# Dilated attention's six query and key projections as three seven-product groups, with their norm weights applied by ScalarE

## What is computed

```python
h = rms_norm_2(x, norm_w)                      # 256 x 1024
q, k, v = h @ w_in[...]                        # each 256 x (3 groups x 8 heads x 64)
q = rms_norm_2(q, q_norm_w)                    # over the 64 channels of a head, weight per group
k = rms_norm_2(k, k_norm_w)
q, k = apply_partial_rope(q), apply_partial_rope(k)   # channels 0 to 15 of 64 are rotated
```

## Time and profile before

| | |
|---|---|
| median of 3 runs | 939.36 us (938.86 to 939.88) |
| the profiled execution's own time | 938.56 us |
| its span in the profile | 936.6 us |
| TensorE matmuls busy | 925.4 us (99%) |
| VectorE busy | 699.5 us (75%) |
| ScalarE busy | 235.3 us (25%) |
| GpSimd busy | 40.6 us (4%) |
| granted TensorE clock | 1.0 of 2.4 GHz |

### The profile page before, as it was taken

One profiled execution on the slowest core, in us unless ns is written; L12 is line 12 of the kernel. 1 busy time (PEld: TensorE's weight loads), 2 busy tenths in 40 slices (PEclk: granted clock), 3 DMA queues, 4 the chain that ended last, 5 costly groups with the idle time before them and its releaser, 6 DMA issues.

```text
span 936.6 us, 12484 instructions
## 1 busy us (share of the span) xinstructions
PE 925.4 (99%) x4976; PEld 583.6 (62%) x4976; DVE 699.5 (75%) x1218; ACT 235.3 (25%) x473; POOL 40.6 (4%) x59
## 2 busy tenths in 40 slices
PE   7999999999999999999999999999999999999998
PEld 5954555945555459999744459457864444469444
DVE  4875965589658677958899763988978789674676
ACT  5314422233333222332100011311103212323210
POOL 0500000000005300000000000000000000000000
PEclk9999999999999999999999999999999999999999
DMA  9753441553527524435555536522424344231721
GB/s 335 243 182 121 149 134 45 180 180 104 189 91 176 185 94 177 142 131 181 180 180 179 179 126 233 181 91 94 177 90 179 111 159 181 94 131 47 269 90 45
DMA packets 51960, 141.77 MB, mean 151 GB/s; under 512 B 4320, under 2 KB 8320, under 8 KB 51648
## 3 DMA queue, kind: packets, MB, share of 16 engines
q1 hardware_dynamic: 49152, 134.55, 40.9%
q0 software_dynamic: 2144, 5.84, 2.6%
q10 hardware_dynamic: 608, 0.61, 0.2%
HBM read 138.89 MB, written 2.10 MB: 151 GB/s over the span
## 4 chain that ended last, share of the span: by engine, by line
PE 98%; DMA 0%; ACT 0%; DVE 0%; issue 0%; DVEq 0%; ACTq 0%
PE pair L2207 34%; PE pair L2292 26%; PE pair L2288 16%; PE pair L2557 6%; PE turned L2148 4%; PE score L2557 3%; PE turned L2557 1%; PE score L2650 1%; PE score L2450 1%; PE score L2466 1%; PE score L2393 1%; PE score L2394 1%; PE score L2719 1%; PE turned L2637 0%; DMA ident<-in_c_ident 0%; PE score L2299 0%
## 5 line engine op out<-in xcount | busy, mean ns | idle before, releaser
L2207 PE MATMUL pair<-ring,hT 128*128 128x512 f32 (+2 forms) x512 | 214.0, 573 | 0.9 <-ACT hT L718 0.9
L1137 DVE TENSOR_TENSOR arena<-arena 128x512 f32<-128x512 f32 (+5 forms) x324 | 192.0, 607 | 17.7 <-PE score L2557 4.1
L2207 PEld LDWEIGHTS pair<-ring,hT 128*128 128x128 f32 x512 | 95.3, 190 | 102.9 <-issue 97.7
L2292 PE MATMUL pair<-ring,arena 128*128 128x512 f32 x192 | 85.8, 594 | 0.0
L2292 PE MATMUL pair<-ring,hT 128*128 128x512 f32 x184 | 83.6, 595 | 0.1
L1137 DVE TENSOR_TENSOR arena<-pair,arena 128x512 f32<-128x512 f32 x60 | 42.3, 705 | 50.0 <-PE pair L2292 26.7
L2292 PE MATMUL pair<-arena 128*128 128x512 f32 x176 | 79.5, 593 | 0.0
L1137 DVE TENSOR_TENSOR arena<-ring 128x2048 f32<-128x2048 f32 (+1 forms) x39 | 72.3, 1854 | 2.2 <-DMA ring<-in_w_ssm_out 0.9
L2207 PE MATMUL pair<-hT,ring 128*128 128x128 f32 (+1 forms) x448 | 72.6, 322 | 0.2 <-ACT hT L714 0.2
L2207 PEld LDWEIGHTS pair<-hT,ring 128*128 128x128 f32 x448 | 64.6, 191 | 6.8 <-ACT hT L714 1.0
L2288 PE MATMUL pair<-arena 128*128 128x128 f32 x544 | 64.0, 276 | 0.0
(11 more groups left out here) (265 smaller groups left out, 1040.1 us busy)
## 6 DMA issues: line engine op xcount, KB each, us to landing
ring<-in_w_in SPq DMA_DIRECT2D x33, 2048.0 KB, 8.3
ring<-in_w_up SPq DMA_DIRECT2D x8, 2048.0 KB, 8.7
ring<-in_w_down SPq DMA_DIRECT2D x8, 2048.0 KB, 7.8
ring<-in_w_o SPq DMA_DIRECT2D x4, 2048.0 KB, 8.5
ring<-in_w_mem_kv SPq DMA_DIRECT2D x2, 2048.0 KB, 7.8
ring<-in_w_glu SPq DMA_DIRECT2D x2, 2048.0 KB, 7.7
ring<-in_w_ssm_out SPq DMA_DIRECT2D x2, 2048.0 KB, 7.9
ring<-in_w_ukv SPq DMA_DIRECT2D x1, 2048.0 KB, 7.8
```

The lines of the kernel that those rows point to most:

```text
L1137: return dve.tensor_tensor(o, a, b, op)
L2207: ins = pe.matmul(o_, s, m, start=a, stop=b)
L2292: ins = pe.matmul(h[bank_], rows[:, k, :], weights[:, k, :], start=not onto and k == 0, stop=k == 3, skip_group_check=True)
```

## The change

The jobs dq0, dq1, dq2, dk0 are gone. In their place stand two more groups, DP (queries of groups 0 and 1) and DQ (queries of group 2, keys of group 0), ahead of DK. The gain of the norm is no longer a pass of VectorE: its weights lie as a column in `stats`, ones in the 16 rotated places, and ScalarE multiplies by them when it copies the transposes out; for the rotated channels VectorE makes tables of cosine and sine times gain once, in 4 small instructions. The gelu's argument takes two passes instead of three. The products with `zs` (`gated_gelu`) and the row sums of GLU move from the projections into the attention's loop, and T1 of GLU moves one step later in that loop.

```diff
-    j += [(f"dq{g}", "w_in_2", C_DQ + DW * g, DW) for g in range(NDIL)]
-    j += [("dk0", "w_in_2", C_DK, DW)]
-    out += halves(DK, C_DK + DW, "w_in_2")
+    out += halves(DP, C_DQ, "w_in_2") + halves(DQ, C_DQ + 2 * DW, "w_in_2") + halves(DK, C_DK + DW, "w_in_2")
...
-ORDERS[GT] = ORDERS[UP] = ORDERS[WP] = (1, 2, 5, 7, 3, 6, 4)
+ORDERS[GT] = ORDERS[UP] = ORDERS[WP] = ORDERS[DP] = ORDERS[DQ] = ORDERS[GLU] = (1, 2, 5, 7, 3, 6, 4)
...
+            for i, name in enumerate(("q_norm_w_2", "k_norm_w_2")):
+                for e in range(2):
+                    pool.dma_start(st[64 * e:64 * e + 64, 380 + 3 * i:383 + 3 * i], d[name].rearrange("o g c -> c (o g)"),
+                                   allow_slow_non_contiguous=True).then_inc(sem("qk_gains_in"), 16)
...
-                    turned((qdT if n < 3 else kdT)[:, 1024 * (n % 3) + 512 * k:1024 * (n % 3) + 512 * k + 512], 512)
+                    turned((qdT if n < 3 else kdT)[:, 1024 * (n % 3) + 512 * k:1024 * (n % 3) + 512 * k + 512], 512, [st[:, 380 + n:381 + n]])
...
+            act.wait_ge(sem("qk_gains"), 2)
             act.wait_ge(sem("z_silu"), 3)
             act.wait_ge(sem("h_ready"), 4 * 8)
...
+            group_copy(DP, 1)
+            group_copy(DP, 5)
+            group_first(DP, raws[1][0][:, 0:512])
...
+            square_pair(DP)
+            group_copy(DQ, 1)
+            group_copy(DQ, 5)
+            turned_dqk(1)
+            turned_dqk(0)
...
+            for k, (trig, lo) in enumerate(((0, 0), (1, 8), (0, 8), (1, 0))):
+                step(tt(turn_tables[:, k], bc(rope[:, trig, :, 32:40].unsqueeze(1), [P, 6, TT, 8]),
+                        bc(qk_gain[:, :, lo:lo + 8].unsqueeze(2), [P, 6, TT, 8]), ALU.mult))
...
-                link(tt(r16, r16, bc(gain[gn][:, DD * g:DD * g + DD].unsqueeze(1), [P, 16, DD]), ALU.mult))
...
                 if m in (5, 6, 7):
+                    if m == 7:
+                        group_rows(DP)
                     z_silu(("zs0", "zs1", "za")[m - 5])
+            group_t1(DP)
             ssm_out(7)
+            group_t3(DP)
             for i in range(2):
...
-                link(tt(z, y, y, ALU.mult))
-                link(dve.tensor_scalar(z, z, 0.044715, 1.0, ALU.mult, ALU.add))
-                mark(tt(z, z, y, ALU.mult), "gelu_z")
+                link(dve.scalar_tensor_tensor(z, y, 0.044715, y, ALU.mult, ALU.mult))
+                mark(dve.scalar_tensor_tensor(z, z, 1.0, y, ALU.add, ALU.mult), "gelu_z")
+            group_t2(DP)
+            group_t4(DP)
+            group_z(DP)
+            group_t1(DQ)
+            group_middle(DP, raws[0][0][:, 0:512], raws[0][0][:, 512:1024])
+            group_last(DP, raws[1][0][:, 512:1024])
+            group_t3(DQ)
...
+                    gated_gelu(0)
                 if s == 1:
                     group_t4(RA)
                     group_z(RA)
                     group_v(RA)
                     group_c22(RA, ra4[3])
-                    group_t1(GLU)
+                    gated_gelu(1)
+                    group_rows(GLU)
                 if s == 2:
                     group_last(RA, ra4[2])
+                    group_t1(GLU)
...
+            for q in (1, 2):
+                group_multiply(DP, q)
             states(7)
+            for q in (5, 7, 3, 6, 4):
+                group_multiply(DP, q)
...
             pe.wait_ge(sem("ssm_taken"), 8)
+            for q in (1, 2, 5, 7, 3):
+                group_multiply(DQ, q)
+            turn_dqk(0)
+            turn_dqk(1)
+            for q in (6, 4):
+                group_multiply(DQ, q)
+            for q in (1, 5, 2, 7):
+                group_multiply(DK, q)
             turn_dqk(2)
...
             turn_dqk(3)
+            for q in (3, 6, 4):
                 group_multiply(DK, q)
```

More of the change, by code:

```diff
@@ L101 @@
 RG, MV, GT, UP = 3, 4, 5, 6
-DK = UP + 4
+DP = UP + 4
+DQ = DP + 1
+DK = DQ + 1
 RS = DK + 1
@@ L182 @@
     "rows_in": "parameters that become columns", "consts_in": "gains, positions and the gate's weight", "masks_in": "masks and levels", "x_out": "x after both branches in DRAM", "x_back": "that x in SBUF again, rows by residue", "near_in": "GpSimd's transfers of the dilated attention's masks", "near_ready": "GpSimd: tiles of those masks, keys by residue",
+    "qk_gains_in": "gains of the dilated attention as columns", "qk_gains": "GpSimd: ones in their rotated places",
     "bgate0": "bias of the even gates", "bgate1": "bias of the odd gates", "ssm_in": "state space parameters",
@@ L203 @@
     "dqk_rows": "one group's queries or keys of the dilated attention",
-    "dk_squared": "ScalarE: squares of the last two groups' keys, third group first",
+    "dk_squared": "ScalarE: squares of a pair of queries or keys, the second of a pair first",
     "angle": "reduced rotary angles", "rope_ready": "ScalarE: cosines and sines",
@@ L634, in _ @@
                                          "p (j c) -> p j c", c=SP_)).then_inc(sem("bexp_ready"), 1)
+            pool.wait_ge(sem("qk_gains_in"), 64)
+            for e in range(2):
+                pool.memset(st[64 * e:64 * e + 16, 380:386], 1.0).then_inc(sem("qk_gains"), 1)
             pool.wait_ge(sem("x_rows"), 6)
@@ L728, in group_copy @@
                     act.wait_ge(sem("second_out"), i)
-                if i >= DK and q == 1:
+                if i >= DP and q == 1:
                     act.wait_ge(sem("last_out"), i)
@@ L1054, in _ @@
             turned_dqk(3)
+            turned_dqk(2)
             group_first(DK, raws[1][0][:, 0:512])
[L1056 to L1061, removed]
+            square_pair(DK)
             group_copy(RS, 1)
@@ L1196, in group_t1 @@
                     dve.wait_ge(sem("group_product"), product_at(MV, 4))
-                elif 0 < i < DK or i in (GLU, SO, WP):
+                elif 0 < i < DP or i in (GLU, SO, WP):
                     dve.wait_ge(sem("group_product"), product_at(i - 1, 6))
@@ L1980, in _, with gated_gelu, pair_roots @@
                 mark(tt(y, y, z, ALU.mult), "gelu_ready")
+            def gated_gelu(i):
+                y, z = uT[:, 1024 * i:1024 * i + 1024], gz[:, 1024 * i:1024 * i + 1024]
                 z, s = (x.rearrange("p (g c u) -> p g c u", g=4, c=4) for x in (z, zs[:, 1024 * i:1024 * i + 1024]))
                 link(tt(z, y.rearrange("p (g u c) -> p g c u", g=4, c=4), s, ALU.mult))
-            dqk(1)
+            def pair_roots(n):
+                dqk_squares(n + 1, raws[0][1], 192)
+                dqk_squares(n, raws[1][1], 208)
+                mean(st[:, 192:224], st[:, 192:224], DD)
+                inverse_root(192, 32)
+            pair_roots(0)
+            dqk_turn(1, raws[0][0], raws[0][1], 224)
+            dqk_turn(0, raws[1][0], raws[1][1], 240)
+            group_t2(DQ)
+            group_t4(DQ)
+            group_z(DQ)
             group_t1(DK)
-            dqk(2)
+            group_middle(DQ, raws[0][0][:, 0:512], raws[0][0][:, 512:1024])
+            group_last(DQ, raws[1][0][:, 512:1024])
             group_t3(DK)
-            dqk(3)
+            pair_roots(2)
+            dqk_turn(3, raws[0][0], raws[0][1], 224)
+            dqk_turn(2, raws[1][0], raws[1][1], 240)
             group_t2(DK)
             group_t4(DK)
+            group_z(DK)
             group_t1(RS)
-            group_z(DK)
-            group_rows(GLU)
+            for i in range(2):
+                gelu(i)
             group_middle(DK, raws[0][0][:, 0:512], raws[0][0][:, 512:1024])
```

90 lines of the change are left out of this document (33 added, 57 removed).

## The result

The change makes the kernel slower: 942.88 us, the median of 6 runs (941.72 to 943.39), against 939.81 (938.86 to 940.22) for the kernel before in as many. The ratio is 1.003, with a 95% interval from 1.002 to 1.004. The forecast was 940.0, in a range that ended at 942.4, and the measured time lies 0.5 above its end. The profiled execution took 942.71 us, its span is 940.7, 4.1 more than before.

A forecast was written before the change was run, and what follows sets the result against it. TensorE's matmuls, busy 99% of the span, were taken to bound the kernel; 6.87 us saved against new waits summed to +0.4, carried through as +0.6, giving 940.0 us, range 937.6 to 942.4.

The forecast's parts named there:

- products: TensorE: 14 half-size products replace 16, at 3.43 us each, minus 6.87 us.
- (a): DP: ScalarE's copy of Q1 before product 2 waits for the third `z_silu`, behind `group_rows(DP)`; plus 2.2 us.
- (b): DP: a chain of VectorE after `states(7)` makes TensorE wait for T2; plus 0.2 us.
- (c): DQ: Q1 must be copied by ScalarE before product 2; plus 0.9 us.
- (d): DQ and DK: eight plus eight transposes on two banks wait for ScalarE's copies; plus 0.65 us twice, 1.3.
- (e): Attention's loop: VectorE's masks free the score banks late at `s` = 2, plus 2.4 us; step 0 plus 0.1.
- (f): GLU: Q1 must be copied before product 2, with only six transposes between; plus 0.2 us.
- I take +0.6: TensorE's clock: no loss priced behind waits of 2.2 and 2.4 us; with the loss, up to +4.4.
- rival 3: TensorE's clock falls behind the waits of 2.2 and 2.4 us: twice 1.9, 943.8 us; chance 5%.
- Rival 1: Most of the saving survives: strided gelu product as fast as a plain one (1.26), (d) hidden; 936.2 us; chance 10%.
- Rival 2: VectorE's chain in DP gives way: new gelu passes as slow as the strided product (2.1 us), 943.4 us; chance 10%.

The follow-up runs named there:

- x4: x3 with group DQ in the order 1, 5, 2, 7, 3, 6, 4 and the paired transposes of DQ and DK each split by a product: 933.53 us.
- x1: The changed kernel with the third `z_silu` moved ahead of `group_rows(DP)` on VectorE: 940.21 us.
- x3: The changed kernel with both VectorE moves, that of x1 and that of x2: 936.08 us, ratio 0.9962 to the kernel before.
- x2: The changed kernel with `group_rows(GLU)` moved one step later in the attention's loop, from `s` = 1 to `s` = 2: 937.76 us, ratio 0.9981 to the kernel before.
- x6: x4 with the block `states(7)` laid between products 1 and 2 of DP: 932.99 us, ratio 0.9929 to the kernel before.
- x7: x3 with the paired transposes of DQ and DK each split by a product, DQ otherwise in the change's own order: 935.34 us.

## Why the prediction was wrong

Term by term, from the timeline of the changed kernel:

| term | forecast | measured | from |
|---|---|---|---|
| products | -6.87 | -6.87 | 3.43 each, as before |
| (a) copy of Q1 of DP | +2.2 | +2.32 | 688.08 to 693.83, less 3.43 |
| clock behind (a) | 0 | +1.77 | 5.20 for 3.43, of which 0.08 is the restart |
| (b) chain in DP | +0.2 | +0.1 | 3.54 for 3.43 at product 6 (the same 0.1 at product 5 stands behind `states(7)` before, too) |
| (c) copy of Q1 of DQ | +0.9 | +1.04 | product 2 at 722.16, 0.96 late, and 3.51 for 3.43 |
| (d) transposes | +1.3 | +1.4 | 2.45 for 1.75, twice |
| (e) score banks, step 0 too | +2.5 | +2.6 | 5.47 between the scores for 2.94; 0.1 |
| clock behind (e) | 0 | +1.66 | 3.48 for 1.82 |
| (f) copy of Q1 of GLU | +0.2 | +0.28 | 0.94 for 0.66 |
| sum | +0.4 | +4.3 | output projections: +4.5; span: +4.1 |

- **The waits were right**, in place, releaser and size: 2.2, 0.9, 0.5 twice and 2.4 were foretold, 2.15, 0.78, 0.43 twice and 2.46 came. They were found by laying the timelines side by side, since the average of VectorE (75% busy) tells nothing of a `z_silu` or a mask that stands 2.9 us too late.
- **The saving of 6.87 us is real.** x4, in which the waits are nearly gone, is 5.1 us under the kernel before by span; 6.87 less 1.24 for the wait of 0.99 in DP with its restart (8.10 for 6.86 from product 1 to the end of product 2), 0.1 of (b), 0.1 of step 0 and 0.28 of (f) is 5.15.
- **The step that failed** is "I take +0.6, since the gaps here are less than half of the 5.34". It took one price at one length, 1.9 us behind an idle stretch of 5.34 us, and read from it that less than half of the length costs nothing. No row supported a bound there. Even the row it leaned on is doubtful: its granted clock reads 1.00 where its matmuls are slow, while behind the waits of the changed kernel the clock rows fall to 0.77 to 0.80. A pause of 2.21 us in the kernel before, with nothing else changed, costs 1.70 us beyond itself. The price worked out for rival 3 (twice 1.9, 943.8) was near the measured 1.77 and 1.66, in part by luck, as the price came from another kind of row; the mechanism of rival 3 is what happened, and its chance of 5% was far too low. Between 0 and 1.9 for each gap the rows of before decide nothing, so both ends belonged into the range, which would then have reached 943.8.
- The Trainium skill, "TensorE: Matmul & The Clock Gate", HAM oscillation, says that a long enough idle gap puts the engine back on half its clock. By that rule, the traces agree: 0.50 behind the pause of 4.21 us. The page asks for a longer gap than the 2.15 to 2.46 us behind which the clock fell here, and there the measurement decides.
- **Rival 1** did not occur: the strided product of the gelu takes about 2.0 us (825.30 to 830.97, less 0.73 for c22 and 2.90 for the rows), not 1.26.
- **Rival 2** did not occur: the new gelu passes take 1.22 to 1.23 us. The chain itself was as tight as foretold: T2 ends at 710.74 and product 6 starts at 710.79.
- **The sign** that the first scores of `s` = 0 start 2.1 to 2.4 us earlier failed: before they start at 797.87, after at 797.65, 0.22 earlier. 1.77 of the difference is the clock behind (a), the rest the excess of (a), (c) and (d). TensorE enters the output projections at 873.00 instead of 868.54, 4.5 us later instead of 0.4 to 0.8. Neither of the two signs that were to show the forecast wrong came: the scores did not start later than before, and the loop did not keep a lead. They watched the waits and could not see this error.
- The two clock losses are also what lets moves of VectorE pay double: x1 removed 1.2 us of waiting and 1.7 of slow matmuls (2.7 by the medians), x3 3.6 and 3.4 (6.8 by the medians).

**Not settled.** No run had an idle stretch between 1.11 and 2.15 us in this part of the program, so nothing is known of what one costs. At 2.2 us the fall seems not to come in every execution (x2); what decides it was not tried, and the pauses were run once each. In 6 of the 44 executions of the kernel before beside the experiments the mean clock is 0.998 too, at spans of 938.8 to 939.6, against 936.3 to 937.3 for those with 1.000; where it falls in those was not profiled. In x3, x4, x6 and x7 no execution is under 0.999.

## What to carry over

In a kernel in which TensorE is never idle, a wait of TensorE can have two prices: its length, and what the matmuls behind it lose if the clock falls (here 1.7 us behind waits of 2.15 and 2.46). Add up the waits that a change creates, then ask of each of the long ones what the second price would be, and keep both answers in the range unless a row of a gap of that length excludes one. The remedy is cheap when another engine's order is written by hand: move the step that makes TensorE wait behind the one that it waits for (two such moves made this change 6.8 us faster), or put a product or a small block between what waits and what it waits for.

## What the runs showed of the hardware

- The granted clock fell behind idle stretches of TensorE of 2.15, 2.21, 2.46 and 4.21 us in the middle of a stream that was otherwise dense, and not behind 0.78, 0.99 and 1.11. The loss in the matmuls behind them was 1.77, 1.70, 1.66 and 2.65 us.
- With one wait of 2.2 us left (x2), 8 of 11 executions had a mean clock of 1.000 and 3 had 0.998. The fall is then not the same in every execution, if the wait was there in all of them, which one profile cannot show.
- A fall during the idle stretch costs nothing until TensorE works again: the pause of 4.21 us lost 3.4 us of full clock in its slices and 2.65 us of time.
- Work without use can pay: four extra instructions in each of the two long waits (x5) kept the granted clock at 1.00 there and made the changed kernel 2.9 us faster.
